# Input projection with a weight's high part times both parts of the tokens in one 512-column pass

## The reference, cut to what matters

```python
h = rms_norm(x, g_pre)                                    # 512 x 2048
proj = einsum('bsd,de->bse', h, w_in)                     # 2048 x 7174
qa, ka, va, ga, qb, kb, vb, gb, fb, qm, gm = split(proj)  # columns of 128 per head
out_a = moba_attention(qa, ka, va, rel_bias)              # 6 heads
log_f = log_sigmoid(fb + b_forget)                        # 6 heads, cumulative bias
out_b = forgetting_attention(qb, kb, vb, log_f)           # 6 heads
km, vm = split(rms_norm(mem, g_mem) @ w_mem_kv)           # 256 memory tokens
out_m = memory_attention(qm, km, vm)                      # 4 heads
y = concat([out_a * silu(ga), out_b * silu(gb), out_m * silu(gm)])
x = x + rms_norm(y @ w_out, g_post)
```

## Time and profile before

| | |
|---|---|
| median of 3 runs | 918.08 us (917.96 to 918.86) |
| profiled execution, its own time | 920.29 us |
| span of the profiled execution | 918.5 us |
| PE busy | 884.9 us, 96% |
| DVE busy | 694.8 us, 76% |
| ACT busy | 503.6 us, 55% |
| POOL busy | 106.1 us, 12% |
| mean granted clock of TensorE | 0.985 of full speed |

### The profile page before, as it was taken

The page is one execution under the profiler, slowest core; times in us unless marked ns, Lnnn a source line. Parts: engine busy times, 40 slices in busy tenths (PEclk is TensorE's granted clock), DMA queues, the critical chain, the costliest instruction groups (busy, mean ns, idle before and its releaser), DMA issues.

```text
span 918.5 us, 16262 instructions
## 1 busy us (share of the span) xinstructions
PE 884.9 (96%) x6525; PEld 841.8 (92%) x6525; DVE 694.8 (76%) x965; ACT 503.6 (55%) x882; POOL 106.1 (12%) x103
## 2 busy tenths in 40 slices
PE   8997998999999999999999999999999999799995
PEld 5887998999999999999999999999999988688884
DVE  4889978987777777777777778787877784975558
ACT  5795554555646464646464646464646474555552
POOL 0000406811111001010021212020202000000000
PEclk9999999999999999999999999999999999899998
DMA  9955476469979566975567774444444496466755
GB/s 299 294 135 151 145 246 194 112 128 201 195 145 197 129 195 133 265 151 142 167 155 160 230 166 111 104 103 105 104 104 104 159 359 225 151 209 198 282 198 184
DMA packets 178641, 161.54 MB, mean 176 GB/s; under 512 B 6969, under 2 KB 143833, under 8 KB 177286
## 3 DMA queue, kind: packets, MB, share of 16 engines
q1 hardware_dynamic: 169574, 142.67, 51.6%
q0 software_dynamic: 8704, 16.78, 12.5%
q10 hardware_dynamic: 288, 1.05, 0.3%
HBM read 152.33 MB, written 43.28 MB: 213 GB/s over the span
## 4 chain that ended last, share of the span: by engine, by line
PE 79%; DVE 13%; ACT 5%; issue 3%; DVEq 0%; POOL 0%; ACTq 0%; POOLq 0%
PE d_ps L630 12%; PE d_ps L632 12%; PE d_ps L631 12%; PE e_ps L630 6%; PE e_ps L632 6%; PE e_ps L631 6%; PE c_ps L630 3%; PE c_ps L632 3%; PE c_ps L631 3%; DVE ring L1394 3%; PE pt_ps L777 3%; PE score_ps L631 1%; PE score_ps L630 1%; PE score_ps L632 1%; DVE sums L1421 1%
## 5 line engine op out<-in xcount | busy, mean ns | idle before, releaser
L1394 DVE TENSOR_TENSOR ring<-raw,ring 128x1024 fp32r<-128x1024 f32 x134 | 165.2, 1237 | 67.9 <-ACT ring L985 67.4
L1394 DVE TENSOR_TENSOR ring<-sums,ring 128x1024 fp32r<-128x1024 f32 x112 | 140.2, 1253 | 96.1 <-ACT ring L985 95.7
L630 PE MATMUL d_ps<-tok_hi,ring 128*128 128x256 f32 x672 | 191.7, 285 | 2.9 <-DVE ring L1394 2.9
L632 PE MATMUL d_ps<-tok_lo,ring 128*128 128x256 f32 x672 | 190.8, 284 | 0.0
L631 PE MATMUL d_ps<-tok_hi,ring 128*128 128x256 f32 x672 | 190.7, 284 | 0.0
L985 ACT ACTIVATE ring<-raw 128x1024 fp32r<-128x1024 f32 x134 | 141.3, 1059 | 72.9 <-PE d_ps L632 46.8
L630 PEld LDWEIGHTS d_ps<-tok_hi,ring 128*128 128x128 f32 x672 | 129.5, 193 | 3.3 <-issue 3.3
L632 PEld LDWEIGHTS d_ps<-tok_lo,ring 128*128 128x128 f32 x672 | 129.6, 193 | 0.0
L631 PEld LDWEIGHTS d_ps<-tok_hi,ring 128*128 128x128 f32 x672 | 129.5, 193 | 0.0
L985 ACT ACTIVATE ring<-sums 128x1024 fp32r<-128x1024 f32 x112 | 117.9, 1053 | 19.8 <-DVE sums L1421 18.1
L1421 DVE TENSOR_TENSOR sums<-raw 128x1024 f32<-128x1024 f32 x56 | 70.2, 1253 | 0.6 <-issue 0.3
(11 more groups left out here) (375 smaller groups left out, 2204.7 us busy)
## 6 DMA issues: line engine op xcount, KB each, us to landing
raw<-in_w_in_dram SPq DMA_DIRECT2D x112, 512.0 KB, 6.2
sum_dram<-in_w_out_dram POOLq DMA_DIRECT2D x32, 512.0 KB, 7.4
raw<-sum_dram SPq DMA_DIRECT2D x32, 512.0 KB, 3.8
raw<-in_w_out_dram SPq DMA_DIRECT2D x24, 512.0 KB, 6.4
raw<-in_w_mem_kv_dram SPq DMA_DIRECT2D x16, 512.0 KB, 8.3
sum_dram<-in_w_out_dram SPq DMA_DIRECT2D x4, 2048.0 KB, 11.9
stage<-in_x_dram SPq DMA_DIRECT2D x4, 1024.0 KB, 9.5
xres<-in_x_dram SPq DMA_DIRECT2D x4, 1024.0 KB, 7.3
```

Source lines behind the costliest of these rows:

```text
L630: pe.matmul(dst, lhs[0], rhs[0], start=start, stop=False, skip_group_check=True)
L632: return pe.matmul(dst, lhs[0], rhs[1], start=False, stop=stop, skip_group_check=True)
L1394: return dve.tensor_tensor(dst, a_, hi_.bitcast(F32), ALU.subtract)
```

## The change: what it does

- **Both token parts in one pass.** `tok_hi` and `tok_lo` become the two halves of one tensor `late`, so that for every operand the high and the low tokens of a tile are one access of 2 x 256. A product is now, for each of the 8 tiles, one pass of 512 columns (high weight x both parts) and one of 256 columns (low weight x high tokens) into the right half of the bank. The right half holds all low terms, the left half high x high.
- **Halves added later.** ACT's copies of A, B and C have 512 columns, as has DVE's subtraction from `e_ps`. For E DVE adds 512 columns to `five` and then its two halves. For D, F and G ACT copies the right half to `one_six` (`low_half`), DVE adds it to the left (`merge`; for v it writes `vT` directly), and ACT and DVE then take the result as before. `last_two` and ACT's copies to `vT` are gone.
- **Waits.** E waits for the subtraction from `e_ps` (before: for the copy of C; F waited for the subtraction). The high parts of q, k and the gate's tanh wait for a merge.
- **Start.** The operand order in the memory stage is dealt anew: DVE and ACT alternate differently between memory tiles and weights, strip 0 starts when the first memory tile is there and waits tile by tile, the clearing of `wf` goes from DVE to GpSimd, the copies of the bias table from DVE to ACT. Late operands are made in the order B, C, E, G, with E and G during pair 0; the last forget gates are computed after product D of pair 0.
- **Forget series.** From DVE's reciprocal on, the series is computed by DVE, one instruction after each product of pairs 2 and 3, instead of by GpSimd.
- **End.** `g_post` is loaded by ACT's queue in step 5 of the output stage, and SP no longer waits there.

```diff
-LATE_ORDER = [TOK_E, TOK_B, TOK_C, TOK_G]
+LATE_ORDER = [TOK_B, TOK_C, TOK_E, TOK_G]
...
+        late, tok_hi_at = place("late", [P, 2, 4, KH, T2], F32R)
+        tok_hi, tok_lo, tok_lo_at = late[:, 0], late[:, 1], tok_hi_at + 4 * 4 * KH * T2
...
+        def halves(bank):
+            return bank[:].rearrange("p (h t) -> p h t", h=2)
+        def both_parts(i):
+            return tok[:, WHOLE[i]] if i in WHOLE else late[:, :, LATE[i]]
...
-            sp.wait_ge(y_raw, NH)
-            sp.dma_start(gpost[:], g_post.partition_broadcast(P)[:, 0, :]).then_inc(gpost_landed, 16)
...
                 if i == TOK_E:
-                    pe.wait_ge(six_taken, p + 1)
-                if i == TOK_F:
                     pe.wait_ge(e_less_six, p + 1)
...
-                hi, lo = token_operand(i)
+                both = both_parts(i)
                 for k in range(KH):
-                    last = three(bank[:, 0:T2], (w[:, 0, k], w[:, 1, k]), (hi[:, k], lo[:, k]),
-                                 i in (TOK_A, TOK_B) and k == 0, k == KH - 1)
+                    pe.matmul(bank[:], w[:, 0, k], both[:, :, k], start=i in (TOK_A, TOK_B) and k == 0, stop=False,
+                              skip_group_check=True)
+                    last = pe.matmul(bank[:, T2:S], w[:, 1, k], both[:, 0, k], start=False, stop=k == KH - 1,
+                                     skip_group_check=True)
...
-            pe.wait_ge(late_ready, 1)
-            forget_gates(2, TOK_E, slice(T2, S), final=True).then_inc(f_done, 1)
...
+                    if p == 0 and i == TOK_D:
+                        pe.wait_ge(late_ready, LATE_ORDER.index(TOK_E) + 1)
+                        forget_gates(2, TOK_E, slice(T2, S), final=True).then_inc(f_done, 1)
...
-                    act.activation(c_ps[:, 0:T2], d, ACTF.Copy, scale=-1.0).then_inc(c_seeded, 1)
+                    act.activation(c_ps[:], d_ps[p % 2][:], ACTF.Copy, scale=-1.0).then_inc(c_seeded, 1)
...
+            def low_half(p, i):
+                n = 3 * p + [TOK_D, TOK_F, TOK_G].index(i)
+                act.wait_ge(used, operand(p, i) + 1)
+                if i == TOK_D:
+                    act.wait_ge(e_less_six, p + 1)
+                elif i == TOK_G:
+                    act.wait_ge(merged, n - 1)
+                bank = {TOK_D: c_ps, TOK_F: e_ps, TOK_G: d_ps[p % 2]}[i]
+                act.activation(one_six[:, int(i == TOK_F)], bank[:, T2:S], ACTF.Copy).then_inc(low_taken, 1)
...
             def before_operand(p, i):
                 take_product(p, i)
+                if i in (TOK_D, TOK_F, TOK_G):
+                    low_half(p, i)
...
-                    dve.tensor_tensor(e_ps[:, 0:T2], e_ps[:, 0:T2], one_six[:], ALU.subtract).then_inc(e_less_six, 1)
+                    dve.tensor_tensor(halves(e_ps), halves(e_ps), one_six[:], ALU.subtract).then_inc(e_less_six, 1)
...
-                    dve.tensor_tensor(last_two[:], d_ps[p % 2][:, 0:T2], five[:], ALU.add).then_inc(last_two_ready, 1)
+                    dve.tensor_tensor(five[:], five[:], halves(d_ps[p % 2]), ALU.add).then_inc(five_added, 1)
+                    dve.wait_ge(five_added, p + 1)
+                    dve.tensor_tensor(five[:, 0], five[:, 0], five[:, 1], ALU.add).then_inc(last_two_ready, 1)
...
+            def merge(p, i):
+                dve.wait_ge(low_taken, 3 * p + [TOK_D, TOK_F, TOK_G].index(i) + 1)
+                bank = {TOK_D: c_ps, TOK_F: e_ps, TOK_G: d_ps[p % 2]}[i]
+                high, low = bank[:, 0:T2], one_six[:, int(i == TOK_F)]
...
+                    dve.tensor_tensor(high, high, low, ALU.add).then_inc(merged, 1)
...
-                    dve.memset(wf[:].bitcast(F32), 0.0).then_inc(wf_cleared, 1)
...
+                if 2 <= p < NM:
+                    forget_series(PRODUCTS * (p - 2) + i)
...
+            pool.memset(wf[:].bitcast(F32), 0.0).then_inc(wf_cleared, 1)
...
-            for c in SERIES[1:]:
-                chain(pool.tensor_scalar(p, p, c, None, ALU.add))
-                chain(pool.tensor_tensor(p, p, s2, ALU.mult))
```

More of the change, by code:

```diff
@@ L1093, in first_strip @@
                 cols = slice(T2 * half, T2 * (half + 1))
-                act.wait_ge(used, operand(p, i) + 1)
                 if p >= NM and (p - NM) % 2:
-                    head = ABHead((p - NM) // 2)
-                    if half == 0:
-                        act.wait_ge(v_turned, head.v)
-                    act.activation(vT[:, cols], bank[:, 0:T2], ACTF.Copy).then_inc(v_copied, 1)
                     return
                 head = MHead(p) if p < NM else ABHead((p - NM) // 2)
+                act.wait_ge(merged, 3 * p + half + 1)
                 if half == 0:
@@ L1190, in _ @@
                     act.activation(kmv[:, 2 * (t - 1)], k_mem[:], ACTF.Copy).then_inc(k_hi, 1)
-                hi_next(1)
+                if t == NM + 1:
+                    for i, (bank, lo_, hi_) in enumerate(table_banks):
+                        act.wait_ge(table_made, i + 1)
+                        act.activation(table[:, lo_:hi_], bank[0:NA, 0:hi_ - lo_], ACTF.Copy).then_inc(table_copied, 1)
                 if t == 0:
@@ L1454, in scale_tile, with lo_memory @@
                 dve.tensor_scalar(one, one, stat[:, 4, t:t + 1], None, ALU.mult).then_inc(tile_scaled, 1)
-            def lo_memory(half):
-                for b in range(4 * half, 4 * half + 4):
+            def lo_memory(b0, b1):
+                for b in range(b0, b1):
                     dve.wait_ge(bank_hi, b + 1)
@@ L1528, in second_strip @@
                 low_cols = slice(S + cols.start, S + cols.stop)
-                src = last_two[:] if late else d_ps[p % 2][:, 0:T2]
+                src = five[:, 0] if late else d_ps[p % 2][:, 0:T2]
                 if p >= NM and (p - NM) % 2 == 0:
@@ L1617, in _ @@
                     minus(kmv[:, 2 * (t - 1) + 1], k_mem[:], kmv[:, 2 * (t - 1)]).then_inc(k_taken, 1)
-                if t > NM:
-                    copy_v_mem(t - 1)
-                for half in range(2):
-                    if t + 1 < STRIPS_MEM:
-                        lo_mem(2 * (t + 1) + half)
-                    else:
-                        add_weights(0, half + 1)
-                        lo_operand(0, half)
-                if t == NM + 1:
-                    for i, (bank, lo_, hi_) in enumerate(table_banks):
-                        dve.wait_ge(table_made, i + 1)
-                        dve.tensor_copy(table[:, lo_:hi_], bank[0:NA, 0:hi_ - lo_]).then_inc(table_copied, 1)
                 if t >= 6:
@@ L1674, in before_operand @@
                     take_product(p, i)
+                if i in (TOK_D, TOK_F, TOK_G):
+                    merge(p, i)
                 if head is not None and not head.memory and p == head.pair_g:
@@ L1687, in after_operand @@
                     second_strip(p, i)
+                if p == 0 and i == TOK_B:
+                    lo_late(TOK_E)
+                if p == 0 and i == TOK_C:
+                    lo_late(TOK_G)
+                if p == 0 and i == TOK_E:
+                    dve.wait_ge(f_low, 1)
+                    dve.scalar_tensor_tensor(out=fbuf[:, 0], in0=f_ps[0:NB, :], scalar=bfor[:, 0:1], in1=fbuf[:, 1],
+                                             op0=ALU.add, op1=ALU.add).then_inc(f_z, 1)
                 if p == 1 and i == TOK_G:
                     dve.wait_ge(f_den, 1)
-                    dve.reciprocal(fbuf[:, 3], fbuf[:, 3]).then_inc(f_rec, 1)
+                    dve.reciprocal(fbuf[:, 3], fbuf[:, 3]).then_inc(f_series, 1)
+                if 2 <= p < NM:
+                    forget_series(PRODUCTS * (p - 2) + i)
                 if p == NM - 1 and i == TOK_G:
```

132 lines of the change are left out of this document (85 added, 47 removed).

## The result

The changed kernel takes 931.56 us (median of 4 runs, 930.66 to 933.41) against 918.47 for the kernel before beside it (917.96 to 921.46): ratio 1.0145, 95% interval 1.0118 to 1.0171. The forecast was 912.6, with a range of 899 to 922: wrong in sign, and outside the range.

The account below looks back on a forecast made before the run. PE's issue was taken to bound the attention pairs. Start -4.0, pairs 1 to 4 +3.2, middle +0.4 and end -5.1 summed to -5.5 us, giving 912.6 against 918.08, with a range of 899 to 922.

Parts of the forecast that it names:

- Pairs 1 to 4: First memory pairs, DVE late: 101.9 us become 105.1, so +3.2, bounds -4 to +8.
- DVE then has 24.5: DVE's work in a memory pair after the change, 24.5 us, against 23.2 of PE work.
- E waits about 4: Pair 2: the 3.3 us reciprocal stands in front as before, so product E waits about 4 us; pair 29.4.
- Passes: Every product: 2.880 us becomes 2.772, 0.108 less, 21.2 us over 196 products if nothing else holds PE.
- The passes give nothing: Rival, all products: a two-half pass costs what two passes did, 2.880 a product; about 931 us; chance 0.05.
- E's wait: Fifth product waits for DVE's subtraction: late by 0.98 us in value/gate pairs, 0.55 in query/key pairs.
- The middle: Pairs 5 to 27: passes -17.4 us, E's waits +17.8, sum +0.4.
- It hides: Pairs 5 to 27: other added work, about 2.2 us of DVE a pair, costs no time; tightest at k's low part.
- Start: Up to pair 1: product A at 89.7 instead of 96.20, pair 1 at 112.3 instead of 116.36: -4.0 us.
- End: Output stage: g_post on ACT's queue shortens PE's wait, -6.6 us; a later last gate +1.5; sum -5.1.
- The chain behind C is longer: Rival, C-to-E chain of every pair: longer than PE can bear, at 0.4 us more about 924; chance 0.19.
- the hidden wait: Rival, E's wait: the subtraction comes in time, middle gains 17.4 and pairs 0 to 4 another 4; about 893; chance 0.12.

Follow-up runs that it names:

- h1: g1 with VectorE's subtraction of C's copy moved back behind the low part of the weights: 922.49 us.
- g1: The changed kernel with subtraction ahead of the low part, reciprocals first in memory pairs, and SyncE's four loads of pair 5 ahead of its waits: 902.84 us.
- e6: The kernel before with only the end's edit: g_post loaded from ScalarE's queue, SyncE no longer waiting there: 914.0 us.
- g4: The kernel before with g_post on ScalarE's queue and the reciprocals first in the memory heads' pairs: 911.42 us.
- h3: g1 with each pass of 512 columns split into two of 256, the bank started once: 914.25 us.
- e2_sub_first: The changed kernel with VectorE's subtraction of C's copy issued ahead of the low part of the weights, TensorE's waits unchanged: 916.51 us.
- f2: e2_sub_first with the forget gates' series back on GpSimd: 915.83 us.
- g2: g1 with a product's eight 512-column passes first, then its eight of 256, instead of in turn: 900.25 us.
- e1: The changed kernel with the old waits: E waits only for ScalarE's copy of C, F for VectorE's subtraction: 917.43 us.
- f1: e2_sub_first with the two reciprocals of memory heads' pairs issued ahead of the low part and the subtraction: 908.96 us.

## Why the prediction was wrong, point by point

**The step that failed** is "Pairs 1 to 4", the +3.2 of "Following both queues: pair 1 25.4, pair 2 29.4, pair 3 26.0, pair 4 24.3". It came to +14.2. The amounts were right: "DVE then has 24.5", and it is busy 24.4, 24.2 and 24.4 us in pairs 1 to 3. What I had too short is the time that DVE stands still beside its work: 1.5 us in my pair 3, and 4.3 in the trace (24.36 busy of 28.67). I took ACT's low-half copy of D as ready when D is. In a memory pair it stands behind ACT's scaling, which waits for reciprocals that DVE issues last, and DVE waits 3.4 us for it and for the high part behind it. The kernel before shows 2.93 us of this wait in each of the four pairs, and I had not read them; the 101.9 from which the forecast counts contains them, my pair times do not. And I left SP out of these pairs: its loads for pair 5 stand behind two waits, and DVE waits 1.98 us for one of them in pair 4 (220.53) of the changed kernel. Of the +14.2 these two orders are 8.5 (113.6 to 105.1, h1) and E's late start is 2.8 (h1 to g1, forecast inside my pair times).

These 8.5 are what the right order saves, and not what the change added: the reciprocals first save 4.0 us in pairs 1 to 3 of the old form too (e6 to g4), and 5.5 in the changed one (86.2 to 80.7, h1). So over these three pairs the changed kernel is 6.8 us longer than before, and still 5.3 with the reciprocals first on both sides. DVE is busy 6.5 us more in them (73.0 against 66.5). That its new work passes into the time almost whole, because its idle time is taken up by such waits, is my reading of these sums; no run takes the merges or the series away and leaves the rest.

The last 2.9 were not tried; 2.6 of them is ACT at the head of pair 1, where the change put the table load and the exponential of the forget gates behind pair 0 and so in front of its gates and of A's copy (116.75, 5.69 after A's first pass; before 3.08):

```profile
113.94 1.28 ACT L1266 ACT_TABLE_LOAD   x1
115.64 0.63 ACT L1266 ACTIVATE fbuf<-fbuf 6x512 f32<-6x512 f32 x1 [0.42 <-POOL fbuf L1965]
```

That this lateness costs PE as much is read from the trace, not shown by a run. My "E waits about 4" in pair 2 was near (3.21).

**Passes.** The second step is the term "8 x (0.2265 + 0.120) = 2.772, 0.108 less". It was mis-sized by over a third: h3 gives 0.068 in the middle, 13.3 us over 196 products by that measure instead of 21.2. In stretches of each head a wide pass and a narrow one take 0.353 us, not 0.3465 (PE rows of e2_sub_first, one product of each kind; the six before 445.46 take 2.12 us from 443.34 on):

```profile
420.93 0.39 PE L682 MATMUL c_ps<-tok,ring 128*128 128x512 f32 x1
421.15 0.28 PE L684 MATMUL c_ps<-tok,ring 128*128 128x256 f32 x1
421.27 0.39 PE L682 MATMUL c_ps<-tok,ring 128*128 128x512 f32 x1
...
445.81 0.40 PE L682 MATMUL d_ps<-late,ring 128*128 128x512 f32 x1
446.04 0.28 PE L684 MATMUL d_ps<-late,ring 128*128 128x256 f32 x1
446.16 0.40 PE L682 MATMUL d_ps<-late,ring 128*128 128x512 f32 x1
```

The wide passes of the output stage, from which I took 0.2265, show one state of the two. The rival "The passes give nothing" falls. By its page's gap (the Trainium skill, TensorE: Matmul & The Clock Gate, Back-to-back issue gap), which the page gives for a single isolated pass, a removed pass would have given 2.5 ns; the measured 0.068 us for 8 removed passes is 8.5 ns each, between that and my 13.

**E's wait.** Right in place and near in size. PE of the changed kernel around it:

```profile
467.09 0.40 PE L682 MATMUL c_ps<-tok,ring 128*128 128x512 f32 x1
...
469.75 0.27 PE L684 MATMUL c_ps<-tok,ring 128*128 128x256 f32 x1
470.76 0.50 PE L682 MATMUL d_ps<-late,ring 128*128 128x512 f32 x1 [0.73 <-DVE e_ps L1541]
471.09 0.28 PE L684 MATMUL d_ps<-late,ring 128*128 128x256 f32 x1
```

From D's first pass to E's first are 3.67 us, less the 2.77 of D 0.90; the first pass behind the wait takes 0.33 instead of 0.23, so 1.0 is lost where I had 0.98. Over a head h1 against g1 gives 1.40 (508.11 - 492.74, over 11), where I had 1.53.

**The middle.** Forecast -17.4 + 17.8 for 23 pairs; measured over 22 by h3, g1 and h1: -9.7 (passes, 502.4 to 492.7) and +15.4 (wait), +5.7 together for a measured +5.3. Two large terms that nearly cancel: an error of a third in one was the whole result here. "It hides" for the rest of the added work held: h3's 45.68.

**Start.** -5.3 for -4.0: PE's first product came at 88.53, where I had 89.7, and pair 0 takes 22.5, my 22.6; G waited 0.58 for the last sum where I had 0.8. The step held. **End.** -3.9 for -5.1, mechanism as told: SP does not wait before these loads, and the clock stays at its upper level: 1.00 in the window that stood at 0.50, and 1.00 from 799 to 804 us, where the same work now lies. PE's long wait of the earlier trace rows has become

```profile
798.68 0.47 PE L636 MATMUL c_ps<-ring,late 128*128 128x512 f32 x1 [1.28 <-issue]
```

and the late gate costs 1.2 (1.4 forecast). e6 has 5.5 for my 6.6.

**The rivals.** "The chain behind C is longer" came nearest in kind, slower than before with DVE and ACT as its place, but its price was put on E's wait in every pair, and the excess lay in the four memory pairs. Its time was 924; 931.6 needed the passes' missing third as well. The range ended at 922 because I bounded pairs 1 to 4 at +8 from amounts of work and from the waits I had found, and the 3.4 us a pair of the circle were not among them.

Three smaller slips of the sums decide nothing: the lower bound of pairs 1 to 4 comes to -5.1 (4 x 23.2 + 4 against 101.9) and not -4, the hidden wait to about 891 (912.6 - 17.8 - 4) and not 893, and the chances outside the range to 0.27 and not 2 in 10.

## What to carry to other kernels

When a change adds an instruction on one in-order queue that reads what another queue has just made, list for both queues everything that stands ahead of the pair, and look for a circle: the amount of work on an engine (here 85% in pairs 1 to 3) does not bound what the circle costs. Look in the trace of before as well: a wait that stands there already (here 2.93 us a pair) is in the time from which a forecast counts, and has to be in the queues that it follows. Before giving up a change that came out slower, ask of each wait whether its releaser can be issued earlier, and give the old kernel the same moves before comparing: here two moves of one or two instructions and one of a queue's loads turned +1.5% into -1.8% with the same work, and the one that moves the reciprocals made the old kernel faster too. A difference of two profiles is one of two executions: where one of them is far from its median (e2's), the medians decide. And where a forecast is the difference of two large terms, give its range the error of each.

## What the runs showed of the hardware

A 1024-wide sum of VectorE takes up to 2.28 us beside GpSimd's 6x512 steps and 1.23 without them, in the same place of the kernel (f2 and e2). VectorE was busy 25.61 us in that pair with the job on GpSimd and 24.19 with the same job in its own queue.

The spacing of wide passes has two values, in stretches of some 10 to 20 us, at a granted clock of 1.00: 0.3465 and 0.353 for a wide and a narrow one. Narrow passes alone keep 0.120 throughout the middle (h3). What sets the two values is open; the order of the widths (g2) is a part of it, 0.2 us a head.

One load of 512 KB, issued in the same place of SP's queue, took 10.6 to 12.3 us to land in four profiles and 15.1 in a fifth (after, e1, f1, f2; e2). The ten runs of e2 lie between 909.1 and 919.6, the four of g1, with the loads first, between 902.8 and 903.7. That the landing makes this spread is likely and not shown: only one execution of each has a trace.
